# Split inputs of blocks one to four: stored by the first stage and loaded by attention, in place of splitting them again

## What is computed

```python
u = rms_norm(h, g_mix); z = u @ w_in                       # 1024 -> q, k, v (512 each), a, b (512 each)
q, k = rms_norm(q) * q_gain, rms_norm(k) * k_gain; glu = a * sigmoid(b)
att = softmax(q k^T / 8 + rel_bias, own chunk of 64 and 8 before) @ v      # 8 heads x 64
cv  = silu(layer_norm(causal depthwise conv of width 31 over glu))         # 512 channels
h = h + concat(att, cv) @ w_out
h = h + (silu(gate) * up) @ w_down                          # FFN, 2816 wide
y = h + sigmoid(rms_norm(h) @ w_ple_gate) * (p @ w_ple_proj)
```

## Time and profile before

| | |
|---|---|
| median of 3 runs | 2774.27 us |
| the profiled execution | 2774.81 us |
| its span in the trace | 2773.1 us |
| TensorE matmuls busy | 2711.6 us, 98% of the span, 14844 |
| VectorE busy | 1675.3 us, 60% |
| ScalarE busy | 1141.6 us, 41% |
| GpSimd busy | 352.2 us, 13% |
| mean granted clock of TensorE | 0.992 |
| HBM traffic | 520.44 MB read, 113.30 MB written, 229 GB/s |

### The profile page before, as it was taken

The page is one execution under the profiler, slowest core; times in us unless marked ns, Lnnn a source line. Parts: engine busy times, 40 slices in busy tenths (PEclk is TensorE's granted clock), DMA queues, the critical chain, the costliest instruction groups (busy, mean ns, idle before and its releaser), DMA issues.

```text
span 2773.1 us, 39376 instructions
## 1 busy us (share of the span) xinstructions
PE 2711.6 (98%) x14844; PEld 2630.8 (95%) x14844; DVE 1675.3 (60%) x3019; ACT 1141.6 (41%) x1895; POOL 352.2 (13%) x182
## 2 busy tenths in 40 slices
PE   7999988999999999999999999999999999999999
PEld 7999988999998999999999999999999999999998
DVE  3455458989888999865555456554556564531223
ACT  5333345666664323344323343233443234432333
POOL 6222221000004555430000000000000000000000
PEclk9999999999999999999999999999999999999999
DMA  4545596776637787786666676766767666866665
GB/s 161 179 148 180 171 312 208 246 229 198 208 127 249 221 255 235 240 274 246 252 241 249 223 272 236 266 228 243 257 247 254 246 244 217 273 227 243 223 248 177
DMA packets 245737, 634.33 MB, mean 229 GB/s; under 512 B 28684, under 2 KB 129676, under 8 KB 245004
## 3 DMA queue, kind: packets, MB, share of 16 engines
q1 hardware_dynamic: 245548, 631.81, 66.6%
HBM read 520.44 MB, written 113.30 MB: 229 GB/s over the span
## 4 chain that ended last, share of the span: by engine, by line
PE 57%; POOL 6%; issue 5%; DVE 1%; ACT 1%; POOLq 0%; DVEq 0%; ACTq 0%
PE psum L187 57%; POOL wres L1739 6%; DVE c_rstd L1813 0%; ACT wres L1639 0%; ACT L1656 0%; PE psum L1923 0%; PE psum L1927 0%; DVE c_g L1890 0%; DVE y L1761 0%; DVE c_cx L1763 0%; ACT c_sd L1656 0%; DVE c_crs L1756 0%; DVE c_up L1892 0%; DVE c_yo L1896 0%; ACT c_sig L1723 0%
## 5 line engine op out<-in xcount | busy, mean ns | idle before, releaser
L187 PE MATMUL psum<-uh,wres 128*128 128x416 f32 x5760 | 1636.2, 357 | 19.4 <-POOL wres L549 9.4
L187 PEld LDWEIGHTS psum<-uh,wres 128*128 128x128 f32 x5760 | 1083.2, 189 | 49.4 <-issue 18.4
L187 PE MATMUL psum<-ul,wres 128*128 128x416 f32 x2880 | 1010.2, 351 | 0.0
L1639 ACT ACTIVATE wres<-x 128x1024 fp32r<-128x1024 f32 (+2 forms) x378 | 434.8, 1150 | 1112.4 <-PE psum L187 1087.7
L187 PE MATMUL psum<-wres 128*128 128x416 f32 x3520 | 686.3, 352 | 6.5 <-POOL wres L1739 3.2
L187 PEld LDWEIGHTS psum<-wres 128*128 128x128 f32 x3520 | 659.0, 188 | 17.3 <-POOL wres L1739 4.6
L187 PEld LDWEIGHTS psum<-ul,wres 128*128 128x128 f32 x2880 | 544.4, 189 | 11.2 <-issue 3.7
L1787 DVE SCALAR_TENSOR_TENSOR y<-c_gw,vec,y 128x416 f32<-128x416 f32 (+1 forms) x600 | 360.9, 668 | 2.8
L1739 POOL TENSOR_TENSOR wres<-x,wres 128x1024 fp32r<-128x1024 f32 (+2 forms) x74 | 202.1, 2732 | 197.6 <-ACT wres L1639 197.6
L1873 DVE TENSOR_TENSOR z<-psum,z 128x416 f32<-128x416 f32 x80 | 47.3, 591 | 191.3 <-PE psum L187 191.3
L1864 DVE TENSOR_TENSOR c_up<-psum,c_rstd 128x416 f32<-128x416 f32 x110 | 65.0, 591 | 150.5 <-PE psum L187 150.4
(11 more groups left out here) (174 smaller groups left out, 2294.5 us busy)
## 6 DMA issues: line engine op xcount, KB each, us to landing
x<-in_w_gu SPq DMA_DIRECT2D x220, 512.0 KB, 3.3
wres<-w_gu_lo SPq DMA_DIRECT2D x176, 512.0 KB, 4.2
x<-in_w_down SPq DMA_DIRECT2D x80, 704.0 KB, 4.1
wres<-w_down_lo SPq DMA_DIRECT2D x64, 704.0 KB, 5.4
x<-in_w_ple SPq DMA_DIRECT2D x40, 640.0 KB, 4.3
w_gu_lo<-wres SPq DMA_DIRECT2D x44, 512.0 KB, 5.1
x<-in_w_in SPq DMA_DIRECT2D x40, 512.0 KB, 4.4
x<-in_w_out SPq DMA_DIRECT2D x40, 512.0 KB, 5.0
```

Source lines behind the costliest of these rows:

```text
L187: mm = nc.tensor.matmul(out, w[wp](kw), u[up](ku), start=first and n == 0 and j == 0, stop=last and n == len(kts) - 1 and j == 2)
L1639: nc.scalar.activation(whi[v % 2][:, 0:kts, :], raw[v % 2][:, 0:kts, :], ACT.Copy).then_inc(hi_done, 1)
```

## The change

`project` stores `uh` and `ul` of blocks 1 to 4 to two tensors in memory, by two DMAs of 1664 KB each, issued right after the load of the next x in unit 1; before the next split ScalarE and VectorE wait for these stores. `attend` no longer loads x and no longer splits it: `u_load` loads a tile of `uh` and one of `ul`, 208 KB each, into one of NX = 10 places (the eight tiles of `uh`/`ul` and two more, `more`), and TensorE waits for them (`u_in`). Tiles 8 to 13 are loaded ahead of the loop, 14 and on inside it, when the last reader of the place is done. `gw0` is loaded in two parts, three channel tiles ahead of the loop and the fourth after its store; the taps start in unit 11 in place of 10. The diff, cut to its core:

```diff
@@ project, sync
                         sp.dma_start(x[:, :, :].rearrange("p k n -> p (k n)"), t["x"][b * P:(b + 1) * P, :]).then_inc(x_in, 16)
+                        rows = slice((ORDER[bi] - 1) * P, ORDER[bi] * P)
+                        for d, u in ((s["uh"], uh), (s["ul"], ul)):
+                            sp.dma_start(d[rows, :], u[:, :, :].rearrange("p k n -> p (k n)").bitcast(F32)).then_inc(st_u, 16)
@@ project, scalar and vector, in unit NU - 1 ahead of split_x
+                    act.wait_ge(st_u, 32 * (bi + 1))
+                    dve.wait_ge(st_u, 32 * (bi + 1))
@@ attend
-    NS, NR, NX = 4, 6, 8
+    NS, NR, NX = 4, 6, 10
-        xk4 = sb("xk", [P, 4, N])
-        xk = [xk4[:, e, :] for e in range(4)] + [z8[:, e, :] for e in (6, 7, 4, 5)]
+        more = sb("more", [P, 4, N], F32R)
+        uh = [c["uh"][:, k, :] for k in range(KD)] + [more[:, e, :] for e in (0, 1)]
+        ul = [c["ul"][:, k, :] for k in range(KD)] + [more[:, e, :] for e in (2, 3)]
-        AHEAD, TAP0 = KD + KD // 2, 10
+        AHEAD, TAP0 = KD + KD // 2, 11
+        def tile_of(v, k):
+            return ((v + 6) // 8) * KD + k
@@ attend, sync
-            def x_load(e):
-                b, k = divmod(e + KD, KD)
+            def u_load(e):
+                b, k = divmod(e, KD)
                 if e >= NX:
-                    sp.wait_ge(u_lo, e - NX + 1)
-                sp.dma_start(xk[e % NX], t["x"][b * P:(b + 1) * P, k * N:(k + 1) * N]).then_inc(x_in[e % NX], 16)
+                    b0, k0 = divmod(e - NX, KD)
+                    if k0 < KD - 1:
+                        sp.wait_ge(u_read, b0 * (KD - 1) + k0 + 1)
+                    else:
+                        sp.wait_ge(used, U0 + 8 * b0 + 2)
+                for place, d in ((uh, s["uh"]), (ul, s["ul"])):
+                    sp.dma_start(place[e % NX].bitcast(F32), d[(b - 1) * P:b * P, k * N:(k + 1) * N]).then_inc(u_in[e % NX], 16)
-            for e in range(3):
-                x_load(e)
             weights(2)
-            for e in range(3, 6):
-                x_load(e)
-            sp.wait_ge(c["first_g"], 16 * (CT - 1))
-            for e in range(6, NX):
-                x_load(e)
+            for e in (KD, KD + 1):
+                u_load(e)
             weights(3)
-            for g in (2, 3):
-                load_queries(sp, c, s, g)
+            load_queries(sp, c, s, 2)
+            for e in range(NX, NX + 4):
+                u_load(e)
+            load_queries(sp, c, s, 3)
             for g in range(2, 8):
                 load_chunk(sp, c, s, 0, g)
             cached(0)
             biases(sp, t, 1, bias[1], bias_in[1])
+            sp.wait_ge(c["first_g"], 16 * (CT - 1))
+            sp.dma_start(gw0[:, 0:CT - 1, :], g_rows[:, 0:CT - 1, 0:HIST + N]).then_inc(gw_in, 16)
@@ in the loop
-                for b, k in reads_done(i - 2):
-                    if (b - 1) * KD + k + NX < (NB - 1) * KD:
-                        x_load((b - 1) * KD + k + NX)
+                for b, k in reads_done(i - 1):
+                    e = (b - 1) * KD + k + NX
+                    if NX + 4 <= e < NB * KD:
+                        u_load(e)
                         if v == 1:
                             sp.wait_ge(st_g[0], 16)
-                            sp.dma_start(gw0[:, :, :], t["o_g"].rearrange("(c p) n -> p c n", p=P)[:, :, 0:HIST + N]).then_inc(gw_in, 16)
+                            sp.wait_ge(gw_in, 16)
+                            sp.dma_start(gw0[:, CT - 1, :], g_rows[:, CT - 1, 0:HIST + N]).then_inc(gw_in, 16)
@@ attend, vector and scalar: split_x and its calls are gone; in tap(n):
+                if n == CT - 1:
+                    dve.wait_ge(gw_in, 32)
@@ attend, tensor, gated(e)
-                u = [lambda k_: uh[:, k_, :], lambda k_: ul[:, k_, :]]
+                u = [lambda k_: uh[tile_of(v, k_) % NX], lambda k_: ul[tile_of(v, k_) % NX]]
                 if v % 8 == 2:
-                    pe.wait_ge(u_lo, v - 2 + k + 1)
+                    e_ = tile_of(v, k)
+                    pe.wait_ge(u_in[e_ % NX], 32 * ((e_ - KD) // NX + 1))
```

More of the change, by code:

```diff
@@ L63, in build @@
             "v2": dram("v2_d", (NT, HEADS * P), F32),
+            "uh": dram("uh_d", ((NB - 1) * P, KD * N), F32), "ul": dram("ul_d", ((NB - 1) * P, KD * N), F32),
             "mh": dram("mh_d", (AW, NT), F32), "ml": dram("ml_d", (AW, NT), F32),
@@ L254, in project @@
         st_qk = [sem("st_q"), sem("st_k")]
+        st_u = sem("st_u")
         st_v, st_vt = [sem("st_v0"), sem("st_v1")], sem("st_vt")
@@ L804, in sem @@
             return ctx.enter_context(nc.semaphore("b_" + name))
-        vec, uh, ul, rstd, y = c["vec"], c["uh"], c["ul"], c["rstd"], c["y"]
+        vec, rstd, y = c["vec"], c["rstd"], c["y"]
         qh2, ql2, k2, v2, kc = c["qh2"], c["ql2"], c["k2"], c["v2"], c["kc"]
@@ L821, in attend @@
         gw0 = sb("gw0", [P, CT, HIST + N])
+        g_rows = t["o_g"].rearrange("(c p) n -> p c n", p=P)
         psum = c["psum"]
@@ L839, in attend @@
         low_dma, OWN = c["low_dma"], 10
-        x_in = [sem(f"x_in{k}") for k in range(NX)]
-        x_hi, u_lo = sem("x_hi"), sem("u_lo")
+        u_in = [sem(f"u_in{k}") for k in range(NX)]
         z_out, tanh_out, glu_out = sem("z_out"), sem("tanh_out"), sem("glu_out")
@@ L1123, in out_low @@
                                         ALU.subtract).then_inc(atl_done, 1)
[L1125 to L1129, removed]
             def evict(v):
@@ L1155, in gated @@
                     evict(v)
-                for b, k in reads_done(i - 1):
-                    split_x(b, k)
             def tap(n):
@@ L1248, in weight_high @@
                 nc.scalar.activation(w_hi[:, v % 2, :, :], w_raw[:, v % 2, :, :], ACT.Copy).then_inc(hi_done, 1)
-            def split_x(b, k):
-                e = (b - 1) * KD + k
-                act.wait_ge(x_in[e % NX], 16 * (e // NX + 1))
-                if k < KD - 1:
-                    act.wait_ge(u_read, (b - 1) * (KD - 1) + k + 1)
-                else:
-                    act.wait_ge(used, U0 + 8 * (b - 1) + 2)
-                nc.scalar.activation(uh[:, k, :], xk[e % NX], ACT.Identity,
-                                     scale=vec[:, V_GMIX + k:V_GMIX + k + 1]).then_inc(x_hi, 1)
             def tanh(p):
```

## The result

| | before | after |
|---|---|---|
| median of 6 runs each, us | 2775.28 (2771.24 to 2780.25) | 2792.20 (2790.02 to 2794.49) |
| ratio, 95% interval | 1 | 1.0059 (1.0048 to 1.0069) |
| span of the profiled execution, us | 2773.1 | 2789.0 |

The changed kernel is 0.6% slower, 2792.2 us where 2790 was forecast. The total fits; three of its terms do not, and they cancel. That the total came within some 2 us is luck in this sense.

The account below looks back on a forecast made before the run. TensorE was taken as the bound (2711.6 of 2773.1 us busy), with VectorE also near its limit in attention. 24.8 + 5.2 - 15 = +15.0 us on 2774.8 gave 2790 us, 0.54% slower, range 2770 to 2808.

Parts of the forecast that it names:

- Part 2: First stage: storing uh and ul delays small transfers and stalls TensorE in four blocks; +24.8 us (12 to 50).
- part 3: Start of attention: late tile 14 holds TensorE, partly offset by the gw0 stall going; +5.2 us (0 to +10).
- part 1: Attention: splits removed from three bunches (stretches where eight tiles were split), 5 us each; -15 us (-7 to -25).
- The delay of the two stores: First stage, SyncE's queue: two large stores landing in issue order push whatever is behind them by 9 us.
- The rival in which the stores pass beside the small ones: First stage: small transfers finish ahead of large stores, so it costs nearly nothing; 2765 us, chance 0.12.
- that of the load's rate: First stage: the two large stores take 15.8 us, +27 in four blocks; 2817 us, chance 0.10.
- the clock: First stage: after each TensorE stall the granted clock is low, losing 2.3 us per stall.
- The landing: Start of attention: tile 14, queued behind the loads issued ahead, lands at 418.7 us.
- The tap: First convolution tap: the wait for gw0 goes, giving back 7.1 us.
- little for shorter units: Attention: a small allowance within the 5 us a bunch, for shorter units at the start of a head pair.
- the rival in which 8.4 us come back: Attention: each bunch gives all it holds, -25 us in all; 2780 us, chance 0.22.
- that of late tiles: Attention: tiles come late in every bunch, 3 to 4 us missing in each of three, +10; 2800 us, chance 0.14.

Follow-up runs that it names:

- experiment 1: Kernel before, with only the eight stores of uh and ul and the two waits on them added; nothing reads them: 2795.78 us, ratio 1.0070.
- experiment 2: Kernel after, with the stores of uh and ul issued in unit 8 in place of unit 1: 2773.74 us, ratio 0.9993.
- experiment 3: Kernel after, with the stores still in unit 1 but issued by ScalarE on its own queue: 2796.29 us, ratio 1.0072 (2 runs).
- experiment 9: Kernel before, with only gw0 loaded in two parts and the taps from unit 11: 2773.72 us, ratio 0.9991.
- experiment 7: Kernel after, stores in unit 8, start loads in order of need, cache and biases of the next head pair in unit 10: 2756.09 us, ratio 0.9927.
- experiment 4: Kernel before, with the store of uh alone added in each block, half the bytes of both stores: 2783.52 us, ratio 1.0029.
- experiment 10: Kernel after without tile loads and their waits; later blocks' gated products read block 0's inputs, so results are wrong: 2775.22 us, ratio 0.9994.
- experiments 8: Kernel before, splits kept and nothing stored, with start loads in order of need and gw0 in two parts: 2773.25 us, ratio 0.9991.

## Why the prediction was right, and where it was not

**In the sum.** 24.8 + 5.2 - 15 = 15.0 was forecast. By the shifts it is 17.85 + 7.0 - 9.5 = 15.4, and 0.5 more behind s135; the medians differ by 16.9. Part 2 was 7 us too dear, part 3 1.8 too cheap, part 1 promised 5.5 too much. The mechanisms of the three parts were right in the main; that their errors cancel to within 1 us was not foreseen.

**Part 2, mechanism.** Right: the stores make the loss of the first stage (experiment 1), and in unit 8 they are free (experiment 2). The delay of the two stores was taken as 9 us; net of the shift of the blocks ahead it is 8.05, 8.57 and 8.65. The ground for it, one queue in order, was too narrow (experiment 3). The rival in which the stores pass beside the small ones is out, and so is that of the load's rate. Of the signs that the prediction named, the waits of 11 to 12 us came; the idle time of 3 to 6 us with a low clock came fully only in block 3: blocks 1 and 2 had 2.6 and 1.8 us, and block 2 no low clock.

**Part 2, size.** By block +4.80, +4.94, +2.11, +6.21 (start of the first normalisation of the next block) for 6.0, 5.7, 5.1, 8.0. The term that was mis-sized most is the clock. It was put at 2.3 us for each of four stalls, 9.2 in all, from the one row behind the 4.32 us stall. By the stretches above the loss is (1 - 0.88) x 14 = 1.7 in block 1, 0.09 x 20 = 1.8 in block 3, none in block 2; in block 0 it is 1.7 around 64, where before had 2.7 (0.81 over the 14 us from 59), so -1.0. That is 2.5. Idle time grew by 3.8, 2.6, 1.8 and 4.8, 13.0 together, for the 15.6 of the prediction: each stall of blocks 1 to 3 was 0.9 to 1.6 us less than forecast, for the delay (0.35 to 0.95 of it) and for 0.6 us of matmuls of the normalisation that TensorE does inside the wait. 13.0 + 2.5 leaves some 2.5 us, of which 1.0 is the late start ahead of any store; the other 1.5 is placed by no row.

**Part 3.** The landing was forecast for 418.7; 436.13 less the shift of 17.85 is 418.3, and the idle time from 421.1 to 436.1 is, less that shift, the one from 402 to 419 that was named as a sign. s9 came 12.8 us later than s0 did, for 12.3 forecast. The tap gave back 5.8 from s12 to s35 instead of 7.1; experiment 9 has 5.8 too. What the prediction did not see is that this step is no price of the tiles but of their place in the queue: experiment 7 turns +7.0 into some -11, 5.8 of it at the tap.

**Part 1.** It was sized at 5 us a bunch from an excess of 3.9 and 5.0 over the plain pace of 2.94 us a unit. Those two rows end at the latest unit of the bunch. The next two units, s40 to s42 and s74 to s76, take 5.02 us each in place of 5.88 and catch up 0.9. Over seven units the excess is 23.64 - 20.6 = 3.0 and 24.75 - 20.6 = 4.2 (4.1 in the fourth bunch), and the gains were 3.0, 3.2 and 3.75: all of the first and most of the others. Part of the gap to the forecast lies in the trace it is measured against: the three bunches together take 73.1 us in the kernel before, 76.5 in experiment 4 with the same attention program, and 63.1 in the kernel after. Against the first the gain is 10.0, against the second 13.5, and 15 was forecast. The "little for shorter units" did not come. After the change the second bunch runs at the plain pace (20.60 / 7 = 2.94), the others at 3.1 and 3.0, and even with no tile loads (experiment 10) a unit needs 2.83 to 3.00. So neither the rival in which 8.4 us come back nor that of late tiles held: late tiles cost 0.9 to 2.6 us, where 10 had been set.

**Left open.** What decides whether the clock falls after an idle time: 3.18 us in block 0 left it at 2.4 GHz, 1.8 us in attention took it to 1.2 GHz, for some 4 us in one kernel and some 10 in another. In experiments 4, 8 and 9 the second bunch is 2.6 to 2.8 us longer than before with such a spell of low clock, with and without an edit in attention, so it is worth a few us either way in any sum here. The medians of experiments 8 and 9 can hold a gain of up to 5 us or none; how often the long bunches come was not measured.

## What to carry to other kernels

Work taken off a busy engine and put into memory paid here only where its bytes found the DMA engines free: the same change was 17 us slower and, with the stores seven units later and the loads in order of need, 19 to 20 faster, about 5 of them from loading `gw0` in two parts. Where a queue is full for tens of us, moving one load ahead can pass the wait to whichever is last (15.0 us for a tile became 13.5 for a weight tile); write down when each is wanted and issue in that order. Before a few us are put down to an edit, compare a stretch of the program that the edit does not touch: here it differed by 3.4 us between two kernels. An excess over a pace is to be read up to the unit where the work has caught up, not up to the latest one.

## What the runs showed of the hardware

- Another engine's queue did not shield small stores from large ones: waits of 9.0, 5.7 and 5.1 us in block 1 with the large stores on ScalarE's queue, 11.1 us with all on SyncE's, and the first stage 22.2 against 17.9 us longer. Two stores of 208 KB took 8.9 and 10.4 us from issue to landing beside the large ones on the other queue, and 2.3 us each where they were issued ahead of the large ones.
- A store of 1664 KB delayed the small one behind it by 3.6 to 4.1 us, two by 8.05 to 8.65. While all else stood, the DMA engines moved 375 GB/s.
- The granted clock after an idle TensorE did not follow the length of the idle time: 1.00 after 3.18 us (block 0) and near 188 us, 0.88 over 14 us around the 1.8 us of block 1, 0.50 for 8 us behind an idle time of 1.82 us in attention (experiment 9), 0.58 over 4 us and then 1.00 behind one of 1.80 us in the same place (the kernel before).
